# Moving the shared down weights into the free third of their slot, and loading a sixth expert's down weights ahead of the routing

## The reference, cut to what matters

```python
y = (silu(h @ w_gate[e]) * (h @ w_up[e])) @ w_down[e]      # a routed expert, on its tokens
shared = (silu(xt @ sh_gate) * (xt @ sh_up)) @ sh_down     # the shared expert, on all tokens
return routed + shared
```

## Time and profile before

| What | Value |
|---|---|
| Time, median of 3 runs | 1320.97 us (1320.21 to 1326.46) |
| The profiled execution's own time | 1319.62 us |
| Its span, first to last instruction | 1317.9 us |
| Mean granted TensorE clock | 0.972 |
| TensorE busy | 1213.0 us, 92% |
| VectorE busy | 576.5 us, 44% |
| ScalarE busy | 373.4 us, 28% |
| Read from HBM | 471.46 MB, 359 GB/s over the span |
| Chain that ended last | TensorE 60%, DMA 29%, SP's queue 5% |

### The profile page before, as it was taken

How to read it: one execution, slowest core, us unless ns; L and a number is a source line. 1 busy time by engine, 2 the same in 40 slices (tenths; PEclk the granted TensorE clock), 3 DMA queues, 4 the chain that set the end, 5 groups by cost and what they waited for, 6 DMA issues and landing times.

```text
span 1317.9 us, 19470 instructions
## 1 busy us (share of the span) xinstructions
PE 1213.0 (92%) x7504; PEld 723.1 (55%) x7504; DVE 576.5 (44%) x1260; ACT 373.4 (28%) x663; POOL 10.0 (1%) x30
## 2 busy tenths in 40 slices
PE   9999999998788988899999998999999788778887
PEld 8986444443344444439999997544444344334443
DVE  6656443333233223328676666734323333333224
ACT  4543222121122222125454444222222221122221
POOL 0000000000000000000000000000000000000000
PEclk9997999999899888899999999999999999999999
DMA  9966999999999999999735436699999999999994
GB/s 304 390 265 242 357 403 420 421 420 421 420 421 420 421 420 421 421 370 401 282 132 192 160 137 251 237 397 422 420 420 420 421 421 420 420 421 421 420 420 183
DMA packets 90464, 473.83 MB, mean 360 GB/s; under 512 B 8321, under 2 KB 23809, under 8 KB 42497
## 3 DMA queue, kind: packets, MB, share of 16 engines
q1 hardware_dynamic: 87440, 465.60, 87.2%
q10 hardware_dynamic: 2928, 6.94, 1.4%
HBM read 471.46 MB, written 1.05 MB: 359 GB/s over the span
## 4 chain that ended last, share of the span: by engine, by line
PE 60%; DMA 29%; SPq 5%; DVE 3%; issue 1%; ACT 1%; ACTq 0%; POOL 0%; DVEq 0%; POOLq 0%
DMA ring<-in_w_up 29%; PE ps L771 20%; PE ps L657 10%; PE ps L669 6%; PE ps L795 6%; PE ps L694 5%; SPq L456 4%; PE ps L751 3%; PE ps L833 2%; PE ps L812 2%; SPq L476 1%; PE ps L841 1%; PE ps L739 1%; PE ps L826 1%; PE ps L954 0%
## 5 line engine op out<-in xcount | busy, mean ns | idle before, releaser
L771 PE MATMUL ps<-ring,xsT 128*32 128x512 f32 (+1 forms) x2432 | 388.5, 612 | 73.9 <-DMA ring<-in_w_up 71.7
L771 PEld LDWEIGHTS ps<-ring,xsT 128*32 128x32 f32 (+1 forms) x2432 | 125.9, 124 | 325.6 <-issue 322.2
L1482 DVE SCALAR_TENSOR_TENSOR sig<-sig,slot_gate,ps 128x256 f32<-128x256 f32 x52 | 25.0, 480 | 386.5 <-ACT sig L1136 386.5
L795 PE MATMUL ps<-ring,hidT 128*32 128x512 f32 (+1 forms) x1216 | 190.1, 597 | 0.5 <-DMA ring<-in_w_down 0.3
L1279 DVE TENSOR_TENSOR ring_low<-ring,wh 128x1024 fp32r<-128x1024 f32 (+1 forms) x112 | 128.6, 1148 | 88.5 <-ACT wh L1060 87.9
L1060 ACT CAST wh<-ring 128x1024 fp32r<-128x1024 f32 (+1 forms) x112 | 110.5, 988 | 150.9 <-PE ps L657 63.7
L1136 ACT ACTIVATE sig<-ps 128x256 f32<-128x256 f32 x52 | 20.0, 384 | 430.8 <-PE ps L771 430.8
L1505 DVE TENSOR_TENSOR X<-X,ps 128x512 f32<-128x512 f32 x184 | 118.3, 682 | 52.3 <-PE ps L812 37.5
L1496 DVE TENSOR_TENSOR yl<-ps,yh 128x512 fp32r<-128x512 f32 x104 | 71.5, 691 | 124.3 <-ACT yh L1145 124.3
L1124 ACT ACTIVATE xsT<-ps,cols 128x256 f32<-128x256 f32 x208 | 102.5, 561 | 69.4 <-PE ps L751 69.4
L1145 ACT CAST yh<-ps 128x512 fp32r<-128x512 f32 x104 | 60.5, 586 | 171.8 <-PE ps L795 152.0
(11 more groups left out here) (202 smaller groups left out, 1282.8 us busy)
## 6 DMA issues: line engine op xcount, KB each, us to landing
ring<-in_w_down SPq DMA_DIRECT2D x128, 1024.0 KB, 25.3
ring<-in_w_gate SPq DMA_DIRECT2D x120, 1024.0 KB, 23.3
ring<-in_w_up SPq DMA_DIRECT2D x120, 1024.0 KB, 25.8
ring<-in_b_w_in SPq DMA_DIRECT2D x8, 3072.0 KB, 16.4
ring<-in_b_w_out SPq DMA_DIRECT2D x4, 3072.0 KB, 10.3
ring<-in_a_w_in SPq DMA_DIRECT2D x9, 1024.0 KB, 11.9
ring<-in_w_gate SPq DMA_DIRECT2D x16, 512.0 KB, 7.3
ring<-in_w_up SPq DMA_DIRECT2D x16, 512.0 KB, 8.1
```

The costliest lines, as they stand in the source:

```text
L771: last = nc.tensor.matmul(ps[first:first + width, p, :], xsT[:, c, p * P + first:p * P + first + width], slot_gu(slot_of(layer, k))[:, c], ...
L795: last = nc.tensor.matmul(ps[first:first + width, 4 + h, :], hidT[:, p, kk * P + first:kk * P + first + width], slot_dn(slot_of(layer, k)) ...
```

## The change

The shared down weights are loaded by SP as a third transfer of the fill "shared", into the last third of its slot; `shared_down` reads them there, and runs in round 2 (inside the combine of unit 4) instead of round 3, ahead of the load that overwrites that third. The buffer `sh_dn` becomes `early_dn` and takes the down weights of expert 5, by the same instruction of ScalarE at the same place. Expert 5 gets a key like those of the known ones and always stands at position 12 (`EARLY`); its gate and up weights are still loaded by SP where position 12 was loaded. SP no longer loads down weights there. The counts of down loads per slot leave position 12 out. VectorE has one more memset and two pairs of small operations at the start, which rewrite `wanted`: positions 7, 8, 9 take places 6, 7, 8 (before: 5, 6, 7), and position 12 takes place 5 (before: 8).

```diff
-FILL_DMAS = {"a_in": 3, "a_out": 1, "b_v": 1, "b_u": 1, "b_out": 1, "shared": 2}
+FILL_DMAS = {"a_in": 3, "a_out": 1, "b_v": 1, "b_u": 1, "b_out": 1, "shared": 3}
...
+EARLY = followers(0, None)[0]
+def down_ready(layer, k):
+    s = slot_of(layer, k)
+    elsewhere = sum(1 for l in range(DEPTH) if slot_of(l, EARLY) == s and (l, EARLY) <= (layer, k))
+    return 16 * (loads_of(layer, k) - elsewhere)
...
-        sh_dn = sb("sh_dn", [P, HC, D])
+        early_dn = sb("early_dn", [P, HC, D])
...
+        def down_of(layer, k):
+            return early_dn if k == EARLY else slot_dn(slot_of(layer, k))
...
                     for lo, w in ((0, sh_gate), (GU // 2, sh_up)):
                         sp.dma_start(ring[:, s, lo:lo + GU // 2], w[j].rearrange("(p c) n -> p (c n)", c=KC)).then_inc(sem, 16)
+                    sp.dma_start(slot_dn(s), sh_down[j].rearrange("(p c) n -> p c n", c=HC)).then_inc(sem, 16)
...
                         sp.wait_ge(W.sh_gu, W.past.sh_gu + TT)
                         for k in followers(layer, None):
                             load_gate_up(layer, k, expert_at(k))
-                            load_down(layer, k, expert_at(k))
...
                 for k in experts_of(u):
-                    pe.wait_ge(dn_load[slot_of(layer, k)], 16 * loads_of(layer, k))
+                    if k == EARLY:
+                        pe.wait_ge(g.early_dn, 16 * (layer + 1))
+                    else:
+                        pe.wait_ge(dn_load[slot_of(layer, k)], down_ready(layer, k))
...
-                                                    slot_dn(slot_of(layer, k))[:, kk, h * HALF:(h + 1) * HALF],
+                                                    down_of(layer, k)[:, kk, h * HALF:(h + 1) * HALF],
...
-                        last = nc.tensor.matmul(dst, sh_hT[:, kk, t * P:(t + 1) * P], sh_dn[:, kk, h * HALF:(h + 1) * HALF],
+                        last = nc.tensor.matmul(dst, sh_hT[:, kk, t * P:(t + 1) * P], slot_dn(s)[:, kk, h * HALF:(h + 1) * HALF],
...
                     if r == 2:
                         pe.wait_ge(W.sh_hT_ready, W.past.sh_hT_ready + 1)
-                        pe.wait_ge(g.sh_dn, 16 * (layer + 1))
-                    shared_part = shared_down if r == 3 else None
+                    shared_part = shared_down if r == 2 else None
...
-                act.dma_start(sh_dn[:], sh_down[layer].rearrange("(p c) n -> p c n", c=HC)).then_inc(g.sh_dn, 16)
+                act.dma_start(early_dn[:], w_down[layer, KNOWN].rearrange("(p c) n -> p c n", c=HC)).then_inc(g.early_dn, 16)
...
-            for n in range(KNOWN):
-                nc.vector.memset(tie_row[:, n:n + 1], 1024.0 * (KNOWN - n))
-            nc.vector.tensor_scalar(tie_row[:, KNOWN:E], minus_i[:, KNOWN:E], 1.0 / P, None, ALU.mult)
+            for n in range(KNOWN + 1):
+                nc.vector.memset(tie_row[:, n:n + 1], 1024.0 * (KNOWN + 1 - n))
+            nc.vector.tensor_scalar(tie_row[:, KNOWN + 1:E], minus_i[:, KNOWN + 1:E], 1.0 / P, None, ALU.mult)
...
+            for half in range(2):
+                places = wanted[half * E:(half + 1) * E, half, :]
+                nc.vector.tensor_scalar(places[:, EARLY - 5:EARLY - 2], places[:, EARLY - 5:EARLY - 2], 1.0, None, ALU.add)
+                step(nc.vector.memset(places[:, EARLY:EARLY + 1], float(KNOWN)))
             for layer in range(DEPTH):
```

More of the change, by code:

```diff
@@ L144 @@
 SLOTS = [slots_in_turn(layer) for layer in range(DEPTH)]
+EARLY = followers(0, None)[0]
+assert all(followers(layer, None) == [EARLY] for layer in range(DEPTH))
+assert all(unit_of(EARLY) == 5 and first_of(2) + 3 == EARLY for layer in range(DEPTH))
+def down_ready(layer, k):
+    s = slot_of(layer, k)
+    elsewhere = sum(1 for l in range(DEPTH) if slot_of(l, EARLY) == s and (l, EARLY) <= (layer, k))
+    return 16 * (loads_of(layer, k) - elsewhere)
 def gate_up_ready(layer, k):
@@ L335, in build @@
         ps = ctx.enter_context(nc.psum_tensor("ps", [P, 8, HALF], FP32))
-        g = sems("g", "xT0 x_in const conv_in rw_in rb_in cols_in ws_in gb_in sb_in rows1 iotas converted rows2 stored sh_dn xT1 first0 first1 first2 first3 first4 first5 first6 first7 first8 "
+        g = sems("g", "xT0 x_in const conv_in rw_in rb_in cols_in ws_in gb_in sb_in rows1 iotas converted rows2 stored early_dn xT1 first0 first1 first2 first3 first4 first5 first6 first7 first8 "
                       "load0 load1 load2 load3 load4 load5 gu0 gu1 gu2 gu3 gu4 gu5 dn0 dn1 dn2 dn3 dn4 dn5 vstep")
```

## The result

The changed kernel takes 1314.12 us (median of 5 runs, 1311.91 to 1315.69) beside 1320.86 us for the kernel before: ratio 0.9948, 95% interval 0.9923 to 0.9974. The forecast was 1316.0 us, range 1312.5 to 1321.0. The profiled execution takes 1314.37 us (span 1312.6) against 1319.62, 5.25 us less, where 4.98 was forecast. The medians lie 6.74 us apart.

The account below looks back on a forecast made before the run. From 278 us on, layer 0 was held to go at the weight stream's pace, 421 GB/s, despite TensorE's 92% busy. Terms: -2.49 - 2.49 + 0 = -4.98 us, from the median 1320.97 to 1316.0 us; range 1312.5 to 1321.0.

Parts of the forecast that it names:

- The term that carries the sum: Weight stream behind the routing: one expert's down load of 1.049 MB leaves it, 2.49 us less per layer at 421 GB/s.
- The terms put at nothing: Shared down load before the routing, shared product in round 2, VectorE's set-up, order of experts: cost 0 each.
- The count of the queue's stock: SP's loads issued since the restart against bytes landed: 1.0 MiB still waits at 245.3 us, so cost 0.
- the push: Moved shared down product delays the refills of units 5 and 6 by 6.9 us; the queue stays filled narrowly, cost 0.
- a restart at 1.2 us: Stream restarting from empty, windows at 166 to 170 us: loses 0.78 and 0.42 us against a full DMA share.
- Rival C: Queue runs dry at the delayed refills of units 5 and 6: +5.6 us per layer, 1332 us; chance 0.05.
- Rival A: Layer 0's last gated products: slow clock after the last wait goes away, 2.5 us more gained, 1313.5 us; chance 0.17.
- the last gated products start at 543.65 (layer 0): End of layer 0's chain of waits: taken as paced by the weight stream, with the slow 9.53 us product on the path.
- 7.0 or 9.5 us: Sign for the faster clock rival: length of the first product after the last wait decides it.
- faster by over 0.5%: Whole kernel: a time under 1314.4 us, chance 0.30.

## Why the prediction was right, and where a step failed

**The term that carries the sum** was right: 2.49 us per layer forecast. The stretches lost 2.2 and 2.5 us in the first pair of traces and 2.5 and 2.4 in the means over the repeats (443.8 to 441.4, 444.3 to 441.9). The load put back took it all away from the stretches, other loads cut by 0.94 MiB ahead of the last gated product were worth 2.2 us each, and behind it nothing. The Trainium skill, "DMA: Bandwidth & Descriptors", section "Where 436 GB/s comes from", has loads from HBM bound at about 358 GB/s per core. The traces differ, and the measurement decides: the plateau is 421 GB/s in every trace of this kernel, which runs on one core.

**The terms put at nothing.** The shared down load, the moved product, the order and the set-up stayed at nothing: the order-only kernel has 1.0001, and the kernel without a moved product has the same stretches. VectorE's second pair ends at 9.0 us, ahead of a split that waits for ScalarE until 9.74. The split started at 9.40 in the first trace of before and at 9.82 in its second, which has no extra set-up, so the set-up is not what moves it (VectorE in the changed kernel, start us, us, what, idle before):

```profile
8.96 0.06 DVE L1738 MEMSET wanted<- 64x1 f32 x1
9.74 1.23 DVE L1295 TENSOR_TENSOR ring_low<-ring,wh 128x1024 fp32r<-128x1024 f32 x1 [0.72 <-ACT wh L1076]
```

**The count of the queue's stock** was right, and doubling the push confirmed its margin: 5.4 us of loss forecast, 6.0 and 4.9 measured. One size in it was low: the prediction took a restart at 1.2 us from the DMA share, but the GB/s of the same two windows (188 and 311 beside 421) make it 1.6 us. Rival C was thus priced properly and rightly held unlikely.

**Rival A had a wrong price.** The step that failed is "the last gated products start at 543.65 (layer 0)", and with it that the slow product there lies on the path and could return 2.5 us. The traces show another gate 30 us later: in the changed kernel the product at 571.39 waits for a load, and in the second trace of the kernel before so does the one at 572.64. In the first trace of before, TensorE came to it at 573.59, when the load had just landed: it was issued at 554.35, and the one up load of this stretch took 19.0 us to land, so it was there at about 573.35 (SP, then the DMA issues from 545 to 580 us).

```profile
554.35 0.38 SPq L456 DMA_DIRECT2D ring<-in_w_up  x1
...
ring<-in_w_up SPq DMA_DIRECT2D x1, 1024.0 KB, 19.0
```

A faster product at 543.65 would have waited there, so by this estimate rival A could return 0.2 us there and not 2.5. Its sign, "7.0 or 9.5 us", could not decide it either: the product took 8.79 us in the changed kernel. TensorE's gate and up product of unit 25 in layer 0, in the changed kernel and in the second trace of before, with what ended the idle time ahead of it:

```profile
571.39 7.09 PE L785 MATMUL ps<-ring,xsT 128*64 128x512 f32 x32 [0.58 <-DMA ring<-in_w_up]
```

```profile
572.64 7.09 PE L771 MATMUL ps<-ring,xsT 128*64 128x512 f32 x32 [0.56 <-DMA ring<-in_w_up]
```

I had read the last DMA link of the chain as the last place at which the stream holds TensorE; it is only the last one in that execution.

**What the medians add.** The changed kernel's medians lie 6.6 to 7.1 us under before's, its mean 5.4. So the first median of 1314.12 falls just under the 1314.4 of "faster by over 0.5%", which had a chance of 0.30, though the mechanism is that of the forecast. What stays open is whether about a microsecond of this is more than scatter. The kernels with the load back in the stream, in its own third and with halves lie 2 to 3.5 us further below before than their stretches explain; one issue less on ScalarE's path is about 1 us of it in the first of them, and no row shows a common cause. The traces do not show one either: outside of the two stretches they have 427.5 to 431.2 us in the four with the load in the stream and 424.3 to 435.1 in the nine without.

## What to carry to other kernels

Where a stream of loads sets the pace, a load was worth its bytes at the stream's rate where it stood between the restart of the stream and the last load that an engine waits for, and nothing behind that; ahead of the routing, where the transfer engines had room, it cost nothing. Idle time ahead of the stream and any free piece of SBUF are where it can go. Before work is moved in front of a refill, count loads issued against bytes landed at that moment: the stock, not the engine's own idle time, says whether the push is free. Judge a gain of a few us by the stretches of the trace that repeat, and keep stages whose clock differs from run to run out of the sum.

## What I had not expected of the hardware

**The routing's length goes with the granted clock of that execution.** The same instructions from 100 to 130 us, first in the changed kernel's first trace, then in the kernel with expert 5 in its own third:

```profile
100.00:115.00 15.00, 12.11 (x56) 10.91 (x55) 9.98 (x17) 7.23 (x12) 1.12 (x2) 0.66 1.00 402
115.00:130.00 15.00, 15.00 (x70) 9.70 (x70) 9.23 (x49) 3.70 (x8) 0.00 (x0) 0.89 0.26 108
```

```profile
100.00:115.00 15.00, 10.95 (x60) 8.26 (x59) 12.21 (x37) 7.16 (x12) 1.11 (x2) 0.89 1.00 402
115.00:130.00 15.00, 15.00 (x81) 9.28 (x79) 7.00 (x29) 4.30 (x9) 0.00 (x0) 1.00 0.26 106
```

The granted clock falls to its lower level (1.2 GHz) for part of the time from 100 to 115 us, in which TensorE is busy for only 11 to 12.6 us of 15. The first gate and up product starts at 129.8 us in the one trace and at 126.6 in the other, although both kernels do nearly the same there. All thirteen traces go this way but one: the four with a clock of 0.89 have 125.3 to 126.6 us, those with 0.81 and 0.73 have 127.8 and 128.8, and the five with 0.66 or 0.67 have 129.7 to 129.9; one with 0.86 has 128.4. Two layers of such a difference are as large as the whole change.

**Half loads are slower than their share tells.** The first window is of the kernel with halves behind unit 2, the second of the changed kernel, in which the halves behind units 0 and 1 land:

```profile
162.00:180.00 18.00, 17.46 (x80) 7.75 (x78) 10.34 (x23) 3.29 (x7) 0.00 (x0) 1.00 1.02 394
```

```profile
140.00:156.00 16.00, 16.00 (x84) 6.90 (x81) 8.00 (x29) 4.24 (x9) 0.00 (x0) 1.00 1.03 411
```

Whole loads have 421 at 1.01. Why the halves differ among themselves no run shows.
